# Compression's first product with the operands swapped: blocks stationary in four column groups, partial sums added and turned by one more product

## The chip, the cores and the metric

One core of one Trainium2 chip runs the whole program. The metric is device time in microseconds. TensorE does the matrix products, VectorE (DVE in rows) and ScalarE (ACT) the elementwise work, GpSimd (POOL) a little of it; SyncE (SP) issues the weight loads.

## The reference, cut to what matters

The program computes two attention layers (`hybrid_layer`), then a second block with a recurrent mixer and 16 experts. The change touches `nsa_compress`, once for keys and once for values in each of the two layers:

```
def nsa_compress(kv, pe, w1, w2):                 # kv: 1 x 256 x 2 groups x 64
    n_c = (S - 32) // 16 + 1                      # 15 blocks of 32 tokens, stride 16
    blocks = kv[:, idx] + pe[None, None, :, None, :]
    blocks = blocks.transpose(0, 1, 3, 2, 4).reshape(B, n_c, G, 32 * 64)
    return jax.nn.silu(blocks @ w1) @ w2          # w1: 2048 x 64, w2: 64 x 64
...
kc = nsa_compress(kvs("nsa_kc"), cmp_pe[0], cmp_w1[0], cmp_w2[0])
vc = nsa_compress(kvs("nsa_vc"), cmp_pe[1], cmp_w1[1], cmp_w2[1])
```

`kc` and `vc` feed the compressed branch of one of the three attention mixers (`s = einsum(qb, kc)`, a masked softmax, `o_cmp`). All is fp32.

## The kernel before, in words

Each engine runs a list of instructions in the order in which `pe_layer`, `v_layer`, `a_layer` and `pool_layer` write them down; they meet only at semaphores. `tick` and `at` name such events; `free(b)`, `fill(b)`, `drain(b)` and `drained(b)` do the same for the eight PSUM banks, so a product into bank b waits until the reader of its last content is done. Weights come as 2 MB units through a ring of four places (more in the expert stage). SP issues them in the fixed order of `unit_order`, and before each it waits until the last product on the unit that held the place is done; `take(pe)` waits for the arrival.

A layer begins with eight groups of projection columns (`cg`), each as two halves of 128 tokens (`pe_in(l, cg, t, w)`), written to banks 4 to 7 and copied to `H` by ScalarE (t=0, `a_h`) and VectorE (t=1, `v_h`). Between them TensorE turns (`pe_turn(n)`) 128x128 pieces through banks `n % 4` (turn 6 through bank 0), which ScalarE (`a_turn`) or VectorE (`v_turn`) copies to `TB`, or, for n=7, to `KC2`. Around the change the orders are:

- TensorE, `cg == 5`: `pe_in` t=0; turns 11, 12, 13; `pe_cmp1`; `pe_in` t=1; turns 3, 4, 5; then gate columns 0 (`pe_gate_cols`), `pe_cmp2`, turn 6, gate columns 1, `pe_cmp_s` (24 small products on `KCT`), then the attention pairs (`pe_attend`).
- VectorE: `v_turn` 7, `v_blocks` (adds `pe`, writes `blk`, which lies in the tile `probs`), `v_turn` 9, `v_rope_q`, `v_turn` 11 and 13, `v_cmp_hid`, `v_h` 5, `v_rope_k`, `v_turn` 3 and 5, top-k (`v_top`), `v_cmp_kv` (writes `KCT` and `VC3`), `v_sel` and so on.
- ScalarE: `a_h` 5, `a_turn` 12, `a_cmp_hid`, `a_turn` 4, `a_gates`, gate tanh 0, `a_turn` 6.

`pe_cmp1` (lines 826 to 834) runs for v = 0 (keys, bank 2) and v = 1 (values, bank 3) 16 products each (`LPAIR`, two tokens of 64 values make the 128 rows). Stationary is `w1[:, v, a, :]`, 128x64, moving is `blk[:, v, a]`, 128x30 (2 groups of 15 blocks), and the output is 64x30, hidden units on partitions. `a_cmp_hid` takes tanh(x/2) of it to `hid`, and `v_cmp_hid` makes (tanh + 1) * x in `hid2`, which `pe_cmp2` multiplies with `w2`; the factor one half comes in `v_cmp_kv`. Bank 3, for v = 1, is that of turn 11, which VectorE reads. The small constant `spread` has, in row s and column c, a one where s mod 32 = c.

A TensorE product of fp32 shows in the trace as two records. All those products go through the helper `mm`, line 648; line 798 is `pe_turn`, line 1247 `v_turn`, line 1577 `a_turn`, line 1590 `a_cmp_hid`, line 1306 `v_cmp_hid`, line 1136 `v_h`, lines 1314 and 1317 `v_cmp_kv`, line 553 SP's load of a unit, line 2181 a product of the expert stage on four column groups (`gates_T`).

Of the kernel before, what the change touches and what calls it, by code (L numbers as in the profile page):

```python
# [8 lines left out]
ALU = mybir.AluOpType  # L9
ACT = mybir.ActivationFunctionType  # L10
# [7 lines left out]
HD = 64  # L18
# [6 lines left out]
N_CMP = (SEQ - CMP_LEN) // CMP_STRIDE + 1  # L25
LPAIR = CMP_LEN // 2
# [12 lines left out]
NSA_MIX = (DSA_H + FOX_H) * HD  # L39
# [183 lines left out]
class Counts:  # L223
# [14 lines left out]
    def tick(self, name, *event, by=1):  # L238

        sem = self.sem(name)  # L240
        self.count[name] += by
        if event:
            self.events[event] = (name, self.count[name])
        return sem, by

    def last(self, name):

        return self.sem(name), self.count[name]

    def at(self, *event):  # L250

        assert event in self.events or not self.events.get("complete"), event
        name, value = self.events.get(event, ("first_building", 1))
        if name.endswith("_filled"):
            self.reading[name] = self.events["use", *event]
        return self.sem(name), value
# [4 lines left out]
    def free(self, b):  # L261

        n = self.uses.get(b, 0)
        self.uses[b] = n + 1
        return self.sem(f"bank{b}_read"), n

    def fill(self, b, *event):

        self.events["use", *event] = self.uses[b]
        return self.tick(f"bank{b}_filled", *event)  # L270

    def drain(self, b, *event):

        use = self.reading.pop(f"bank{b}_filled", None)
        assert use or not self.events.get("complete"), (b, event)
        self.done[b] = use or 1
        if event:
            self.events[event] = (f"bank{b}_read", self.done[b])
        return self.sem(f"bank{b}_read"), 1

    def drained(self, b):

        return self.sem(f"bank{b}_read"), self.done[b]


def build(nc, A, out, events):
    ctx = ExitStack()
    with ctx:
# [3 lines left out]
        def sb(name, *shape, dt=F32, stack=ctx):  # L292
            return stack.enter_context(nc.sbuf_tensor(name, [P, *shape], dt))
# [15 lines left out]
        def C(name, rows=slice(0, P)):  # L309
            lo, hi = CF[name]  # L310
            return const[rows, lo:hi]
# [59 lines left out]
        def row_of(r):  # L371
# [3 lines left out]
        PCT = rot[:, :, :].rearrange("p t n -> p (t n)")[:, 2816 - 512:2816].rearrange("p (n s) -> p n s", s=P)  # L375
        Zc = wide[:, 1, NSA_MIX:NSA_MIX + GROUPS * TILES * HPG * N_CMP].rearrange(
            "p (g t j c) -> p g t j c", g=GROUPS, t=TILES, j=HPG)
        mx = sb("mx", 3, 2, 2, stack=one)
        den = sb("den", 3, 2, 2, stack=one)
        rin = sb("rin", 3, 2, 2, stack=one)  # L380
# [266 lines left out]
        def mm(pe, o, a, b, start, stop):  # L647
            return pe.matmul(o, a, b, start=start, stop=stop)  # L648
# [177 lines left out]
        def pe_cmp1(pe, l):  # L826
            pe.wait_ge(*at("cmpw", l))
            pe.wait_ge(*at("blocks", l))
            for v in range(2):
                pe.wait_ge(*free(2 + v))  # L830
                for a in range(LPAIR):
                    ins = mm(pe, bank[2 + v][0:HD, 0:2 * N_CMP], w1[:, v, a, :],
                             blk[:, v, a, :, :].rearrange("p g c -> p (g c)"), a == 0, a == LPAIR - 1)
                ins.then_inc(*fill(2 + v, "cmp1", l, v))

        def pe_cmp2(pe, l):
            pe.wait_ge(*free(2))
            pe.wait_ge(*at("hid", l, 0))
            mm(pe, bank[2][0:HD, 0:2 * N_CMP], w2[0:HD, 0, :], hid2[0:HD, 0, :], True, True)
            pe.wait_ge(*at("hid", l, 1))  # L840
            for g in range(GROUPS):
                ins = mm(pe, bank[2][0:N_CMP, 64 * (g + 1):64 * (g + 2)], hid2[0:HD, 1, g * N_CMP:(g + 1) * N_CMP],
                         w2[0:HD, 1, :], True, True)
            ins.then_inc(*fill(2, "cmp2", l))
# [155 lines left out]
        def pe_layer(pe, l):  # L1000
            if l == 0:
                pe_open(pe)
            for cg in range(0 if l else 2, 6):
                w = take(pe, WIDTHS[cg])
                pe_in(pe, l, cg, 0, w)
                if cg == 0:
                    pe_xT(pe, l, 1)
                if cg == 3:
                    pe_index(pe, l, 0)
                if cg == 4:  # L1010
                    pe_cum(pe, l)
                if cg == 5:
                    for n in (11, 12, 13):
                        pe_turn(pe, l, n)
                    pe_cmp1(pe, l)
                pe_in(pe, l, cg, 1, w)
                if cg == 2:
                    for n in (0, 1, 2):
                        pe_turn(pe, l, n)
                    pe_gate(pe, l)  # L1020
                if cg == 3:
                    pe_index(pe, l, 1)
                if cg == 4:
                    for n in (7, 8, 9, 10):
                        pe_turn(pe, l, n)
                if cg == 5:
                    for n in (3, 4, 5):
                        pe_turn(pe, l, n)
            w = take(pe)
            pe_gate_cols(pe, l, 0, w)  # L1030
            pe_cmp2(pe, l)
            pe_turn(pe, l, 6)
            pe_gate_cols(pe, l, 1, w)
            pe_cmp_s(pe, l)
            pe_attend(pe, l, take(pe))
# [152 lines left out]
        def v_rope_k(dve, l):  # L1188
            dve.wait_ge(*at("h", l, 5, 0))
            rope(dve, COL["ks"], GROUPS, 32, plain(RKS, GROUPS, 32))  # L1190
            rope(dve, COL["kw"], GROUPS, 32, plain(RKW, GROUPS, 32), "rope", l, "k")
# [53 lines left out]
        def v_turn(dve, l, n):  # L1245
            def copy(o, i, s):
                return dve.tensor_scalar(o, i, s, None, ALU.mult) if s != 1.0 else dve.tensor_copy(o, i)  # L1247
            turn_read(dve, copy, l, n)
# [51 lines left out]

        def v_cmp_hid(dve, l):

            for v in range(2):
                dve.wait_ge(*at("hid_tanh", l, v))
                dve.wait_ge(*at("cmp1", l, v))
                dve.scalar_tensor_tensor(hid2[0:HD, v, :], hid[0:HD, v, :], 1.0,
                                                   bank[2 + v][0:HD, 0:2 * N_CMP], ALU.add, ALU.mult).then_inc(*drain(2 + v, "hid", l, v))
                dve.wait_ge(*drained(2 + v))

        def v_cmp_kv(dve, l):  # L1310
            dve.wait_ge(*at("cmp2", l))
# [176 lines left out]
        def v_layer(dve, l):  # L1488
            if l == 0:
                v_window(dve, 0)  # L1490
                for half in range(2):
                    v_ada_rows(dve, 0, half)
                    v_ada_open(dve, half)
                    v_uT(dve, 0, 0, half)
                dve.wait_ge(*at("consts", 1))
                dve.wait_ge(*at("params", 1))
            else:
                v_uT(dve, l, 1)
            v_h(dve, l, 0)
            if l:  # L1500
                dve.wait_ge(*at("lngb", l - 1))
                v_rows(dve, l, 0)
            v_h(dve, l, 1)
            if l:
                v_rows(dve, l, 1)
            else:
                v_ada_gate(dve)
            v_rope_dsa(dve, l)
            v_h(dve, l, 2)
            v_turn(dve, l, 1)  # L1510
            v_gate(dve, l)
            v_h(dve, l, 3)
            v_fox_z(dve, l)
            v_index(dve, l)
            v_top(dve, 0, P, TOPK // 8 - 2)
            v_fox_cum(dve, l)
            v_top(dve, 0, P, 2)
            v_h(dve, l, 4)
            v_turn(dve, l, 7)
            v_blocks(dve, l)  # L1520
            v_turn(dve, l, 9)
            v_rope_q(dve, l)
            v_turn(dve, l, 11)
            v_turn(dve, l, 13)
            v_cmp_hid(dve, l)
            v_h(dve, l, 5)
            v_rope_k(dve, l)
            v_turn(dve, l, 3)
            v_turn(dve, l, 5)
            v_top(dve, P, 384, TOPK // 8)  # L1530
            v_cmp_kv(dve, l)
            v_sel(dve, l)
            v_gT(dve, l, 0)
            v_cmp_z(dve, l)
            v_gT(dve, l, 1)
            if l + 1 < DEPTH:
                v_window(dve, l + 1)
            else:
                v_mod_window(dve)
            v_attend(dve, l)  # L1540
            v_ln(dve, l)
# [45 lines left out]
        def a_cmp_hid(act, l):  # L1587
            for v in range(2):
                act.wait_ge(*at("cmp1", l, v))
                act.activation(hid[0:HD, v, :], bank[2 + v][0:HD, 0:2 * N_CMP], ACT.Tanh, scale=0.5).then_inc(*tick("scalar_step", "hid_tanh", l, v))  # L1590
                act.wait_ge(*last("scalar_step"))

        def a_gates(act, l):
            act.wait_ge(*at("h", l, 5, 1))
# [1585 lines left out]
```

## Time and profile before

| | |
|---|---|
| Median of the runs | 1201.88 us (1199.24, 1201.88, 1205.79) |
| The profiled execution | 1202.91 us, span 1201.10 us, mean granted clock 0.939 |
| TensorE matmul busy | 1027.3 us (86%), 7706 records |
| TensorE weight load busy | 534.7 us (45%) |
| VectorE busy | 428.0 us (36%) |
| ScalarE busy | 236.9 us (20%) |
| GpSimd busy | 54.2 us (5%) |
| HBM read | 321.47 MB, 269 GB/s over the span |

The span is from the first to the last instruction of the profiled execution, and 1.81 us lie around it. A busy share is a mean over stages with different limits; which instructions set the end is told by the chain that is followed back from the last instruction, and by the timelines around the place of the change. A form such as `128*64 128x30` gives the stationary block's rows and columns and then the moving block. A bracket at the end of a row gives the engine's idle time before it and what ended that.

### The profile page before, as it was taken

To read this page: it belongs to the slowest core of one execution; us is meant where nothing else is said; L and a number is where in the kernel's file an instruction comes from. 1 tells how busy PE (TensorE), PEld (TensorE's weight loads), DVE (VectorE), ACT (ScalarE), POOL (GpSimd) and SP (SyncE) were. 2 spreads that over 40 slices of the span, in tenths; PEclk is the share of its full clock that TensorE was granted. 3 is DMA by queue.
4 is the path that set the end of the run, shared out by engine and by line. 5 is a ranking of instruction groups with operands and counts; after the bars stand their busy time and mean duration, and the time that the engine had idled before them with its cause. 6 is when DMAs were issued, how large, how long until landed. Compare 5 with 4: busy or idle time off the path is not lost.

```text
span 1201.1 us, 18162 instructions
## 1 busy us (share of the span) xinstructions
PE 1027.3 (86%) x7706; PEld 534.7 (45%) x7706; DVE 428.0 (36%) x1023; ACT 236.9 (20%) x587; POOL 54.2 (5%) x70
## 2 busy tenths in 40 slices
PE   5999999999999989999988889998666666666667
PEld 2344774444477446885657765432111111111112
DVE  0137646333775527445238783411000000000002
ACT  0011135111213423444113352200000000000002
POOL 0101000000100000000222400000000000000000
PEclk9999989999999999999999999899888888879779
DMA  9973238553325994013222016999999999999996
GB/s 383 404 280 141 86 133 331 188 193 141 140 78 225 426 385 165 1 70 141 81 98 108 5 72 244 411 416 432 428 431 430 428 431 431 429 430 429 431 429 275
DMA packets 28159, 323.68 MB, mean 269 GB/s; under 512 B 3264, under 2 KB 3392, under 8 KB 5808
## 3 DMA queue, kind: packets, MB, share of 16 engines
q1 hardware_dynamic: 26048, 314.18, 63.8%
q0 software_dynamic: 2032, 8.35, 2.0%
q8 instruction: 61, 1.00, 0.3%
q14 instruction: 18, 0.15, 0.0%
HBM read 321.47 MB, written 1.05 MB: 269 GB/s over the span
## 4 chain that ended last, share of the span: by engine, by line
PE 60%; DMA 31%; DVE 4%; issue 2%; ACT 1%; SPq 1%; DVEq 0%; ACTq 0%
PE banks L648 49%; DMA zuv_to_Kt<-in_stream 17%; DMA ring<-in_stream 14%; PE banks L659 3%; PE banks L2195 1%; PE banks L911 1%; PE banks L897 1%; PE banks L932 1%; SPq L553 1%; PE banks L894 1%; PE banks L798 1%; DVE KC L1247 0%; PE banks L902 0%; PE banks L935 0%; DVE probs L1297 0%
## 5 line engine op out<-in xcount | busy, mean ns | idle before, releaser
L648 PE MATMUL banks<-ring,uT 128*128 128x512 f32 (+1 forms) x512 | 226.4, 597 | 7.2 <-DMA ring<-in_stream 4.2
L648 PEld LDWEIGHTS banks<-ring,uT 128*128 128x128 f32 x512 | 96.3, 192 | 121.6 <-issue 112.5
L648 PE MATMUL banks<-ring,scr_qk 128*32 128x512 f32 (+1 forms) x496 | 86.6, 655 | 23.2 <-DMA ring<-in_stream 22.7
L648 PE MATMUL banks<-ring,UWK 128*32 128x512 f32 (+1 forms) x336 | 87.8, 795 | 15.9 <-ACT UWK L3051 9.3
L648 PE MATMUL banks<-scr_qk 64*64 64x64 f32 (+2 forms) x2368 | 80.4, 260 | 21.8 <-DMA scr_qk<-in_stream 15.4
L2761 DVE SCALAR_TENSOR_TENSOR UWK<-UWK,banks 128x256 f32<-128x256 f32 x16 | 6.7, 421 | 259.0 <-ACT UWK L3043 259.0
L3043 ACT ACTIVATE UWK<-banks 128x256 f32<-128x256 f32 x16 | 6.1, 383 | 361.2 <-PE banks L648 361.2
L648 PEld LDWEIGHTS banks<-scr_qk 64*64 64x64 f32 (+2 forms) x2368 | 54.6, 132 | 46.3 <-issue 34.6
L648 PE MATMUL banks<-UWK,ring 128*128 128x256 f32 x320 | 71.0, 380 | 0.0
L648 PEld LDWEIGHTS banks<-UWK,ring 128*128 128x128 f32 x320 | 60.4, 190 | 9.3 <-issue 1.4
L2195 PE MATMUL banks<-UWK 128*128 128x512 f32 x128 | 63.7, 620 | 0.9 <-DVE UWK L2769 0.9
L648 PE MATMUL banks<-uT,ring 128*128 128x256 f32 x256 | 59.3, 392 | 0.0
L659 PE MATMUL banks<-ring,KC 128*32 128x512 f32 x384 | 47.3, 617 | 13.8 <-DMA ring<-in_stream 13.8
L648 PEld LDWEIGHTS banks<-ring,scr_qk 128*32 128x32 f32 (+1 forms) x496 | 24.5, 124 | 72.9 <-issue 47.2
L648 PEld LDWEIGHTS banks<-ring,UWK 128*32 128x32 f32 (+1 forms) x336 | 27.3, 152 | 61.2 <-issue 49.9
L648 PEld LDWEIGHTS banks<-uT,ring 128*128 128x128 f32 x256 | 50.2, 199 | 7.1
L2769 DVE TENSOR_TENSOR UWK<-banks,grow 128x512 f32<-128x512 f32 x16 | 11.1, 692 | 109.7 <-PE banks L648 109.7
L1616 ACT ACTIVATE probs<-banks,mx 128x128 f32<-128x128 f32 x88 | 36.6, 418 | 41.9 <-DVE mx L1384 37.9
L2195 PEld LDWEIGHTS banks<-UWK 128*128 128x128 f32 x128 | 21.8, 190 | 47.4 <-issue 45.1
L1136 DVE COPY H<-banks 128x512 f32<-128x512 f32 (+1 forms) x12 | 8.2, 681 | 84.5 <-PE banks L648 84.5
L648 PE MATMUL banks<-const,scr_qk 64*64 64x64 f32 (+1 forms) x208 | 20.2, 448 | 20.9 <-DMA misc<-in_stream 20.9
L648 PE MATMUL banks<-Vt_to_O,UWK 128*64 128x128 f32 (+1 forms) x208 | 23.1, 504 | 9.2 <-DVE Vt_to_O L2524 2.7
(380 smaller groups left out, 1223.6 us busy)
## 6 DMA issues: line engine op xcount, KB each, us to landing
ring<-in_stream SPq DMA_DIRECT2D x93, 2048.0 KB, 14.4
scr_qk<-in_stream SPq DMA_DIRECT2D x11, 2048.0 KB, 40.1
Vt_to_O<-in_stream SPq DMA_DIRECT2D x11, 2048.0 KB, 39.6
zuv_to_Kt<-in_stream SPq DMA_DIRECT2D x10, 2048.0 KB, 40.1
scr_qk<-in_stream SPq DMA_DIRECT2D x11, 1024.0 KB, 40.9
wide<-in_stream SPq DMA_DIRECT2D x10, 1024.0 KB, 38.5
const<-in_stream SPq DMA_DIRECT2D x10, 1024.0 KB, 37.4
misc<-in_stream SPq DMA_DIRECT2D x10, 1024.0 KB, 39.6
```

The source lines that it names most:

```text
L553: sp.dma_start(held(slot[k]), A["stream"][k, :, :]).then_inc(*tick(f"arrived{slot[k]}", by=16))
L648: return pe.matmul(o, a, b, start=start, stop=stop)
L659: ins = pe.matmul(bank[b][32 * j:32 * j + 32, :], window[:, j * (DCH // 4) + k, lo:lo + 32], w[:, j * (DCH // 4) + k, :], start=(n, k) == ...
L798: ins = pe.transpose(bank[b][0:rows, (2 * m + t) * P:(2 * m + t + 1) * P], f(t), ident)
L894: pe.matmul(bank[b + s][:, 0:P], q[:, 0:P], k[:, 0:P], start=True, stop=False)
L897: pe.matmul(bank[b + s][:, P:384], q[:, P:SEQ], k[:, :], start=False, stop=False)
L911: ins = pe.transpose(bank[4 + s][:, i * P:(i + 1) * P], probs[:, m % 3, s, i * P:(i + 1) * P], ident)
L932: pe.matmul(bank[6][HD * s:HD * s + HD, 0:SEQ], H[:, 0, v:v + HD], probT[:, m % 2, s, 0:SEQ], start=first and kind != "slc", stop=False)
L1136: dve.tensor_copy(H[:, 1, AT[cg]:AT[cg] + WIDTHS[cg]], bank[b][:, 0:WIDTHS[cg]]).then_inc(*drain(b, "h", l, cg, 1))
L1616: ins = act.activation(probs[:, i, s, lo:hi], bank[b + s][:, lo:hi], ACT.Exp, bias=mx[:, i, s, t:t + 1], accum_out=den[:, i, s, t:t + 1])
L2195: ins = pe.matmul(bank[2 * t + h], PgT[:, t, :], ye[:, h, 0:512], start=e == 0, stop=e == EXPERTS - 1)
L2769: dve.tensor_tensor(ye[:, 0, 0:512], bank[4], grow[:, 0:512], ALU.mult).then_inc(*drain(4, "ye", e, 0))
```

## The change

`pe_cmp1` swaps the operands. Stationary is now a block of 32 columns of the flat `probs` (the 30 of `blk[:, v, a]` and the first two of the next, 30 only for the very last), moving is `w1[:, v, a, :]`, 64 columns. Product a goes to column group j = a % 4, so to partitions 32j to 32j+31 of the bank and its columns 0 to 63, and four products add up in each group. The output has blocks on partitions and hidden units along them, in four partial sums. ScalarE copies both banks to `cmp_part` (in the tile `wide`). A new product, `pe_cmp1_sum`, for each v has `cmp_part[:, v, :]` stationary (128x64) and 30 columns of `spread` moving: that adds the four parts and turns the result, so that it is 64x30 again, for both v in bank 2 (`hid_rows`). TensorE runs it between the second half of the projection and turns 3 to 5. The tanh and the (tanh + 1) * x are one instruction each now, over both v; the tanh waits for the sum, and `v_cmp_hid` moves behind `v_rope_k`. No DMA is added, removed or moved.

```diff
@@ -375,6 +375,8 @@
         PCT = rot[:, :, :].rearrange("p t n -> p (t n)")[:, 2816 - 512:2816].rearrange("p (n s) -> p n s", s=P)
         Zc = wide[:, 1, NSA_MIX:NSA_MIX + GROUPS * TILES * HPG * N_CMP].rearrange(
             "p (g t j c) -> p g t j c", g=GROUPS, t=TILES, j=HPG)
+        cmp_part = wide[:, 1, NSA_MIX:NSA_MIX + 2 * HD].rearrange("p (v n) -> p v n", v=2)
+        hid_rows = bank[2][0:HD, 0:64].rearrange("p (v n) -> p v n", v=2)[:, :, 0:2 * N_CMP]
         mx = sb("mx", 3, 2, 2, stack=one)
         den = sb("den", 3, 2, 2, stack=one)
         rin = sb("rin", 3, 2, 2, stack=one)
@@ -829,15 +831,24 @@
             for v in range(2):
                 pe.wait_ge(*free(2 + v))
                 for a in range(LPAIR):
-                    ins = mm(pe, bank[2 + v][0:HD, 0:2 * N_CMP], w1[:, v, a, :],
-                             blk[:, v, a, :, :].rearrange("p g c -> p (g c)"), a == 0, a == LPAIR - 1)
+                    j, r = a % 4, a // 4
+                    lo = (v * LPAIR + a) * 2 * N_CMP
+                    n = 2 * N_CMP if (v, a) == (1, LPAIR - 1) else 32
+                    ins = mm(pe, bank[2 + v][32 * j:32 * j + n, 0:HD], pflat[:, lo:lo + n], w1[:, v, a, :],
+                             r == 0, r == LPAIR // 4 - 1)
                 ins.then_inc(*fill(2 + v, "cmp1", l, v))
+
+        def pe_cmp1_sum(pe, l):
+            pe.wait_ge(*free(2))
+            for v in range(2):
+                pe.wait_ge(*at("cmp_part", l, v))
+                ins = mm(pe, bank[2][0:HD, 32 * v:32 * v + 2 * N_CMP], cmp_part[:, v, :], C("spread")[:, 0:2 * N_CMP], True, True)
+            ins.then_inc(*fill(2, "cmp_sum", l))
 
         def pe_cmp2(pe, l):
             pe.wait_ge(*free(2))
-            pe.wait_ge(*at("hid", l, 0))
+            pe.wait_ge(*at("hid", l))
             mm(pe, bank[2][0:HD, 0:2 * N_CMP], w2[0:HD, 0, :], hid2[0:HD, 0, :], True, True)
-            pe.wait_ge(*at("hid", l, 1))
             for g in range(GROUPS):
                 ins = mm(pe, bank[2][0:N_CMP, 64 * (g + 1):64 * (g + 2)], hid2[0:HD, 1, g * N_CMP:(g + 1) * N_CMP],
                          w2[0:HD, 1, :], True, True)
@@ -1024,6 +1035,7 @@
                     for n in (7, 8, 9, 10):
                         pe_turn(pe, l, n)
                 if cg == 5:
+                    pe_cmp1_sum(pe, l)
                     for n in (3, 4, 5):
                         pe_turn(pe, l, n)
             w = take(pe)
@@ -1300,12 +1312,10 @@
 
         def v_cmp_hid(dve, l):
 
-            for v in range(2):
-                dve.wait_ge(*at("hid_tanh", l, v))
-                dve.wait_ge(*at("cmp1", l, v))
-                dve.scalar_tensor_tensor(hid2[0:HD, v, :], hid[0:HD, v, :], 1.0,
-                                                   bank[2 + v][0:HD, 0:2 * N_CMP], ALU.add, ALU.mult).then_inc(*drain(2 + v, "hid", l, v))
-                dve.wait_ge(*drained(2 + v))
+            dve.wait_ge(*at("hid_tanh", l))
+            dve.wait_ge(*at("cmp_sum", l))
+            dve.scalar_tensor_tensor(hid2[0:HD, :, :], hid[0:HD, :, :], 1.0, hid_rows, ALU.add, ALU.mult).then_inc(*drain(2, "hid", l))
+            dve.wait_ge(*drained(2))
 
         def v_cmp_kv(dve, l):
             dve.wait_ge(*at("cmp2", l))
@@ -1522,9 +1532,9 @@
             v_rope_q(dve, l)
             v_turn(dve, l, 11)
             v_turn(dve, l, 13)
-            v_cmp_hid(dve, l)
             v_h(dve, l, 5)
             v_rope_k(dve, l)
+            v_cmp_hid(dve, l)
             v_turn(dve, l, 3)
             v_turn(dve, l, 5)
             v_top(dve, P, 384, TOPK // 8)
@@ -1587,8 +1597,10 @@
         def a_cmp_hid(act, l):
             for v in range(2):
                 act.wait_ge(*at("cmp1", l, v))
-                act.activation(hid[0:HD, v, :], bank[2 + v][0:HD, 0:2 * N_CMP], ACT.Tanh, scale=0.5).then_inc(*tick("scalar_step", "hid_tanh", l, v))
-                act.wait_ge(*last("scalar_step"))
+                act.activation(cmp_part[:, v, :], bank[2 + v][:, 0:HD], ACT.Copy).then_inc(*drain(2 + v, "cmp_part", l, v))
+            act.wait_ge(*at("cmp_sum", l))
+            act.activation(hid[0:HD, :, :], hid_rows, ACT.Tanh, scale=0.5).then_inc(*tick("scalar_step", "hid_tanh", l))
+            act.wait_ge(*last("scalar_step"))
 
         def a_gates(act, l):
             act.wait_ge(*at("h", l, 5, 1))
```

## Rows read from the trace of the kernel before

**Rows 1.** The page, chain that ended last, shares by engine and line.

```profile
PE 60%; DMA 31%; DVE 4%; issue 2%; ACT 1%; SPq 1%; DVEq 0%; ACTq 0%
```

**Rows 2.** The chain in order of time: start us, us, what.

```profile
122.10 0.70 DVE TB L1247
122.84 8.26 PE banks L648 x48
131.10 1.31 PE banks L798 x12
...
840.65 5.91 SPq L553
```

**Rows 3.** TensorE timeline, layer 0: start us, us, engine, line, what.

```profile
120.49 2.05 PE L648 MATMUL banks<-probs,w 128*64 128x30 f32 x32
122.84 2.05 PE L648 MATMUL banks<-probs,w 128*64 128x30 f32 x32 [0.30 <-DVE TB L1247]
124.82 6.28 PE L648 MATMUL banks<-ring,uT 128*128 128x448 f32 x16
...
139.25 0.30 PE L648 MATMUL banks<-hid,w 64*64 64x30 f32 x2
139.48 0.39 PE L648 MATMUL banks<-w,hid 64*15 64x64 f32 x4
139.80 0.66 PE L798 MATMUL banks<-const,rot 128*128 128x128 f32 x4
...
147.30 2.43 PE L648 MATMUL banks<-KCT,TB 64*128 64x15 f32 x24
```

**Rows 4.** TensorE timeline, the same place in layer 1.

```profile
334.04 2.05 PE L648 MATMUL banks<-probs,w 128*64 128x30 f32 x32 [0.29 <-DVE TB L1247]
336.02 6.28 PE L648 MATMUL banks<-ring,uT 128*128 128x448 f32 x16
```

**Rows 5.** Busy time by stretch, the last stretch: stretch, length, engines, clock, DMA, GB/s.

```profile
840.00:1201.00 361.00, 244.74 (x1488) 63.97 (x1480) 31.77 (x60) 19.84 (x50) 0.00 (x0) 0.84 0.98 417
```

**Rows 6.** Waits of the SP queue, 440 to 850: us, times, longest.

```profile
SPq L553 <- PE banks L648: 284.0, 28, 48.2
```

**Rows 7.** TensorE timeline, a burst of the expert stage.

```profile
773.33 0.65 PE L2181 MATMUL banks<-const,scr_qk 128*32 128x128 f32 x16
```

**Rows 8.** Groups by line and form, TensorE: busy us, mean ns, idle before.

```profile
L2181 PE MATMUL banks<-const,scr_qk 128*32 128x128 f32 x256 | 10.0, 273 | 0.0
...
L648 PE MATMUL banks<-KCT,TB 64*128 64x15 f32 x48 | 4.9, 260 | 0.0
```

**Rows 9.** ScalarE timeline, layer 0.

```profile
122.62 1.28 ACT L1590 ACT_TABLE_LOAD   x1 [1.81 <-PE banks L648]
...
124.99 0.19 ACT L1590 ACTIVATE hid<-banks 64x30 f32<-64x30 f32 x1 [0.89 <-PE banks L648]
132.07 0.60 ACT L1577 ACTIVATE TB<-banks 128x512 f32<-128x512 f32 x1 [6.90 <-PE banks L798]
```

**Rows 10.** VectorE timeline, layer 0.

```profile
124.20 0.18 DVE L1306 SCALAR_TENSOR_TENSOR hid<-hid,banks 64x30 f32<-64x30 f32 x1 [0.69 <-ACT hid L1590]
...
131.21 0.62 DVE L1136 COPY H<-banks 128x448 f32<-128x448 f32 x1 [5.76 <-PE banks L648]
...
135.29 1.42 DVE L1247 TENSOR_SCALAR TB<-banks 128x512 f32<-128x512 f32 x2
...
145.74 0.36 DVE L1314 TENSOR_SCALAR KCT<-banks 64x15 f32<-64x15 f32 x2
```

**Rows 11.** Busy time by stretches of 1 us, columns as in rows 5.

```profile
150.00:151.00 1.00, 1.00 (x6) 0.91 (x5) 0.90 (x5) 0.00 (x0) 0.00 (x0) 0.50 0.84 360
...
156.00:157.00 1.00, 1.00 (x4) 0.84 (x3) 0.00 (x0) 0.08 (x1) 0.00 (x0) 0.65 0.00 0
```

**Rows 12.** Busy time by stretches of 10 us, columns as in rows 5.

```profile
120.00:130.00 10.00, 9.70 (x84) 6.94 (x82) 3.69 (x10) 2.25 (x4) 0.00 (x0) 1.00 0.01 2
...
360.00:370.00 10.00, 10.00 (x48) 8.48 (x47) 4.39 (x16) 2.29 (x9) 0.78 (x1) 0.83 0.78 295
```

## The prediction

> **What bounds the kernel now.** I read the chain that ended last first, since the change touches two short stretches and the question is whether they lie on it. TensorE has 60% of it, the weight stream 31%, VectorE 4% [rows 1]. In order of time the chain goes, in layer 0, from VectorE's read of turn 11 (122.10, 0.70 us) to 48 TensorE records from 122.84 on [rows 2]. By TensorE's timeline these 48 are 32 of the second compression product (v=1) and 16 of the second half of the sixth projection group [rows 3]. So only v=1 is on the chain. v=0 starts at 120.49 and is done by 122.54; then TensorE waits 0.30 us for bank 3, which VectorE empties at 122.80. Whatever v=0 saves is added to that wait. Layer 1 has the same pattern 211.2 us later: v=1 at 334.04, the projection at 336.02 [rows 4].
>
> The second question is whether time won there reaches the end. The end is bound by the stream: from 840 to 1201 us the 16 DMA engines are busy 0.98 of the time, TensorE 245 of 361 us [rows 5]. But SP issues each load only when a ring place is free, and what it waits for is TensorE: 284.0 us in 28 waits between 440 and 850 [rows 6], and the chain itself passes through such an SP issue at 840.65 [rows 2]. No clock time is fixed after the compression; every load behind it is released by a program event that moves with TensorE. So a gain is passed on nearly whole, and a loss too. It is only small beside the span.
>
> **What v=1 costs, before and after.** Before: v=1 starts at 122.84 and the projection behind it at 124.82, 1.98 us for 32 records (16 fp32 products, two records each), 62 ns a record; 1.98 us in layer 1 as well [rows 3, 4]. Each has 64 stationary columns and 30 moving ones. After: again 16 products in 32 records, each with 32 stationary columns and 64 moving ones, four column groups in turn. The trace has no such form. The nearest is the expert stage's small burst on four column groups, 32 stationary and 128 moving: 16 records in 0.65 us, the mean duration of one 0.273 us, so starts lie (0.65 - 0.27) / 15 = 25 ns apart [rows 7, 8]. That is far under what 128 columns cost alone: the 12 full-width transposes of turns 3 to 5, 128 columns each, take 1.31 us on the chain, 109 ns each [rows 2]. So four groups do stream side by side. With half the moving columns the spacing should be no longer, but here each product also brings new weights, where the burst repeats one block on four groups. Bounds: 25 ns below (the burst), 62 ns above (the present form, which has twice the stationary columns and no overlap of groups). I take 30, near the burst, because it shares the groups and the stationary width. v=1 then takes 32 x 30 = 0.96 us, 1.02 less than now. At 25 it is 1.18 less, at 62 nothing.
>
> A rule speaks against this. The Trainium skill, TensorE: Matmul & The Clock Gate, section "The mechanism" (Part 3), says that a weight load overlaps matmuls in flight only where the row group differs, and all four column groups here use the same 128 rows. By its "LDWEIGHTS" section a load of 32 columns is an estimated 27 ns, and a record would take that and its streaming in series, about 80 ns; the sum by it is 32 x 80 = 2.6 us, 0.6 more than now, against my 1.0 less. The burst's 25 ns [rows 7] disagrees for repeated weights.
>
> **The added summing product.** `pe_cmp1_sum` puts four records (two products, 64 stationary and 30 moving columns, the old form) between the projection and turns 3 to 5, on the chain. At 62 ns they are 0.25 us. They also change the array's tiling twice. The nearest row is the second compression product: six small records with both changes of tiling take from 139.25 to 139.80, 0.55 us [rows 3]. Bounds 0.25 and 0.55; I take 0.40, since four of six records are there with both changes. Their waits cost nothing: v=1's copy out of PSUM by ScalarE is at most a 0.2 us instruction (0.19 us for the tanh of 30 columns [rows 9], 64 columns are a little more, say 0.22) and is done by about 124.1, and the projection covers it until 130. If that cover were gone, the sum would wait some 0.3 us.
>
> **ScalarE.** Two copies are added, two tanhs become one, and the tanh moves behind the sum: it waits until about 130.5 (turn 3 starts at 131.10 now [rows 2], so the sum at 130.08, and it takes 0.40). In front of it stands the table load, 1.28 us, which before fell at 122.62 in ScalarE's idle time. Table load and a tanh of 60 columns (0.25 us) end at about 132.1; then comes turn 4's read, which ran at 132.07 before [rows 9] and could now run at 131.5, were ScalarE free. So it stays where it was; the next who needs it is turn 6 on bank 0, TensorE at 139.80, 7 us later. Behind it come `a_gates` and the first gate tanh, which waits for gate columns that TensorE finishes before 139.25 [rows 3], so they have the same cover. Nothing is late.
>
> **VectorE.** `v_cmp_hid` leaves the idle stretch after turn 13 (its two instructions were 0.18 us each) and becomes one instruction over 64x60 behind `v_rope_k`, in VectorE's busiest stretch: 0.2 us, with its wait and hand-over 0.25. It needs the tanh (132.1) and comes at about 134.3, so it does not wait. Queued behind it are turns 3 and 5 (135.29), top-k and `v_cmp_kv`; the last KCT write ends at 146.10 [rows 10]. TensorE begins the products on KCT at 147.30, a margin of 1.20 us [rows 3]. VectorE's stretch starts at the copy of the projection (131.21 [rows 10]), which moves 1.02 earlier with TensorE; less 0.25 it is 0.77 earlier. TensorE arrives 0.62 earlier. The margin becomes 1.35; it would decide only if the new VectorE work cost over 1.6 us. `pe_cmp2` needs the result at about 138.6, 4 us after it is there. POOL and SP get no new work. `cmp1`, for which POOL's next load of `w1` waits, comes earlier, with a layer between.
>
> **Sum.** Per layer 0.40 - 1.02 = -0.62 us; two layers -1.2. The profiled execution took 1202.91 us, 1.81 over its span of 1201.10, and it is 1.03 over the median of 1201.88. Span 1199.9, own time 1201.7, median 1200.7. By the bounds, the best is 2 x (0.25 - 1.18) = -1.9 (1200.0) and the worst 2 x 0.55 = +1.1 (1203.0).
>
> **Rivals.**
> (1) Weight loads and matmuls of the four groups run in series, so that nothing overlaps. From rows: 128 stationary and 15 moving columns take (2.43 - 0.26) / 23 = 94 ns in the KCT product [rows 3, 8], 64 and 30 take 62. Taking off the streaming (0.85 ns a column, from 109 ns for 128) leaves 81 and 36 ns of load, so 32 columns perhaps 16, and 64 moving columns add 54: 70 ns. v=1 is 2.24 us, with the sum +0.66 a layer: 1203.2. The four-group burst at 25 ns is against it. 10%. The rule of the Trainium skill above would bring this case about.
> (2) The clock falls inside the compression; this one ends slower. The granted clock is 1.00 (2.4 GHz) now through 120 to 130 us. But after the 24 tiny KCT products that begin at 147.30 it is 0.50 (1.2 GHz) from 150 on and back within 156 to 157 (0.65, so at about 156.7), and in layer 1 there is a shorter drop (0.83 over 360 to 370, 3.4 us of it low) [rows 11, 12]. After the change v=0 ends at about 121.6, TensorE is idle for 1.2 us, then works for 1 us in small matmuls: less work in the array than before. If the clock falls for 6.7 us over the projection, 3.4 us are lost. In one layer 1204.1, in both 1207.5. It decides from the first such drop, since 3.4 is over five times the gain of a layer. Against it: the present 4.3 us with a wait trigger none. 10%, of which 4 for both.
> (3) The drops at 150 and 361 us go away, because TensorE's pattern before them moves: 3.4 + 1.7 = 5.1 us won, 1195.6. The KCT burst just ahead of both is unchanged, which speaks against. 8%.
> (4) The gain is absorbed by a wait that I don't see, in the mixed stretch of 160 to 430 us, where a load may come as late as before: 1201.9. The loads there are released by TensorE too. 10%.
>
> **How the numbers follow.** The forecast holds 62%: 1200.7, its own range 1197.5 to 1204.0, the bounds (1200.0 to 1203.0) and some of the scatter of the runs shown, 1199.24 to 1205.79. For 8 in 10 I take 1196.5 to 1205.5, which takes in rivals 1 and 4 and the one-layer case of 2, and leaves out two-layer drops and rival 3. About 0.5%, 6 us, is what a measurement of this kernel can tell from no change. Faster by more needs rival 3 and luck: 5%. Slower by more needs rival 2 in both layers, or scatter on one: 6%. Within: 89%.
>
> **What would show it.** In the changed profile: v=1 starts where turn 11's read ends, its 32 records of 128*32 take 0.8 to 1.2 us, and the wait before it grows from 0.30 to about 1.2; four records of form 128*64 stand before turn 3, 0.3 to 0.5 us from the projection to turn 3; the table load stands after the sum, and turn 4's read directly behind the tanh; VectorE's hid instruction follows rope without idle time; `KCT` is still ready before TensorE asks. From the start of v=1 to the start of the KCT products, now 24.46 us, I expect 23.8. Records over 62 ns, a granted clock under 1.00 from 120 to 140, or an idle TensorE ahead of the sum would make the prediction wrong.

## The result, and the profile after

The changed kernel takes 1197.25 us (median of 20 executions, 1192.05 to 1203.51), the kernel before 1205.22 (20 executions, 1199.24 to 1209.32). The ratio is 0.9941, 95% interval 0.9928 to 0.9954. That is inside the range of the forecast (1196.5 to 1205.5), but it is 7 us of gain where I had worked out 1.2, and it lies just beyond the half per cent, where I had given 5%.

That the time lies inside the range is luck. I worked from a median of 1201.88 of three executions, and twenty executions of the same kernel have 1205.22. Measured from 1201.88, the range allows a gain of at most 5.4 us; by the ratio the gain is 7.1 (5.5 to 8.7), so it lies outside. My 1.2 us taken off 1205.22 would have been 1204.0.

The profile after has the same chain as before, share by share, TensorE 60% and the stream 31% [rows 1]. TensorE's timeline of it in layer 0, in the columns of [rows 3] (line 650 is the helper `mm`, line 800 the turns):

```profile
120.62 0.65 PE L650 MATMUL banks<-w,probs 128*32 128x64 f32 x32
122.98 0.65 PE L650 MATMUL banks<-w,probs 128*32 128x64 f32 x32 [1.70 <-DVE TB L1259]
123.56 6.28 PE L650 MATMUL banks<-ring,uT 128*128 128x448 f32 x16
129.77 0.42 PE L650 MATMUL banks<-const,wide 128*64 128x30 f32 x4
130.12 0.87 PE L800 MATMUL banks<-const,rot 128*128 128x128 f32 x6
...
146.53 2.43 PE L650 MATMUL banks<-KCT,TB 64*128 64x15 f32 x24
```

v=1's 32 records run from 122.98 to the projection at 123.56: 0.58 us against 1.98, or 18 ns a record with the hand-over to the projection. Before it TensorE waits 1.70 us instead of 0.30, so v=0's gain is lost there as expected. The sum takes 0.35 us (129.77 to 130.12). From v=1's start to the KCT products it is 23.55 us, before 24.46 [rows 3]: 0.91 us won in this layer. The repeated profile of the changed kernel (`e4_after_again`) has 23.56 us in layer 0, where 23.5 was expected.

In layer 1 of the same execution the 1.4 us of v=1 are eaten up by the clock:

```profile
333.24 0.65 PE L650 MATMUL banks<-w,probs 128*32 128x64 f32 x32 [1.70 <-DVE TB L1259]
333.82 7.98 PE L650 MATMUL banks<-ring,uT 128*128 128x448 f32 x16
341.73 0.42 PE L650 MATMUL banks<-const,wide 128*64 128x30 f32 x4
```

The projection takes 7.91 us here instead of 6.21 in layer 0. Busy time by stretch says why; the column before the last two is the granted clock, 1.00 in layer 0 and 0.83 in layer 1, which is 3.4 us of the ten at the lower level (1.2 GHz):

```profile
120.00:130.00 10.00, 8.30 (x91) 4.60 (x88) 3.49 (x10) 2.35 (x5) 0.00 (x0) 1.00 0.00 0
...
330.00:340.00 10.00, 8.30 (x85) 4.68 (x84) 3.69 (x9) 2.61 (x5) 0.00 (x0) 0.83 0.00 0
```

ScalarE in layer 0 (line 1600 the new copy, 1602 the tanh, 1587 a turn's read; compare [rows 9]):

```profile
123.70 0.22 ACT L1600 ACTIVATE wide<-banks 128x64 f32<-128x64 f32 x1 [2.07 <-PE banks L650]
123.94 1.28 ACT L1602 ACT_TABLE_LOAD   x1
130.23 0.21 ACT L1602 ACTIVATE hid<-banks 64x60 f32<-64x60 f32 x1 [5.00 <-PE banks L650]
131.31 0.60 ACT L1587 ACTIVATE TB<-banks 128x512 f32<-128x512 f32 x1 [0.87 <-PE banks L800]
```

VectorE in layer 0 (line 1148 the projection's copy, 1317 `v_cmp_hid`, 1259 turn 3 and 5, 1324 KCT; compare [rows 10]):

```profile
129.95 0.62 DVE L1148 COPY H<-banks 128x448 f32<-128x448 f32 x1 [6.31 <-PE banks L650]
...
134.03 0.21 DVE L1317 SCALAR_TENSOR_TENSOR hid<-hid,banks 64x60 f32<-64x60 f32 x1
134.27 1.42 DVE L1259 TENSOR_SCALAR TB<-banks 128x512 f32<-128x512 f32 x2
...
144.73 0.36 DVE L1324 TENSOR_SCALAR KCT<-banks 64x15 f32<-64x15 f32 x2
```

The two profiled executions have spans of 1201.10 and 1200.4 us. They differ by 0.7 us where the medians differ by 8 (the profiled execution of the changed kernel, 1202.21 us, is the second slowest of its 20), so this pair alone can't show where the time came from. The question for the experiments was why a cut of about 2 us on the chain is worth 7.

### The profile page after: what moved, and what is told of

It is laid out like the page before. It is cut to its first block, busy times and chain, and to the rows that moved or that the text cites. A ratio compares the mean times of both kernels' runs of the same rounds, so it can differ in the third digit from the quotient of the medians.

```text
span 1200.4 us, 18176 instructions
## 1 busy us (share of the span) xinstructions
PE 1018.7 (85%) x7714; PEld 530.7 (44%) x7714; DVE 428.3 (36%) x1021; ACT 237.5 (20%) x589; POOL 54.3 (5%) x70
## 3 DMA queue, kind: packets, MB, share of 16 engines
HBM read 321.47 MB, written 1.05 MB: 269 GB/s over the span
## 4 chain that ended last, share of the span: by engine, by line
PE 60%; DMA 31%; DVE 4%; issue 2%; ACT 1%; SPq 1%; DVEq 0%; ACTq 0%
PE banks L650 49%; DMA zuv_to_Kt<-in_stream 17%; DMA ring<-in_stream 14%; PE banks L661 3%; PE banks L2207 1%; PE banks L922 1%; PE banks L908 1%; PE banks L943 1%; SPq L555 1%; PE banks L905 1%; PE banks L800 1%; DVE KC L1259 0%; PE banks L913 0%; PE banks L946 0%; DVE probs L1309 0%
## 5 line engine op out<-in xcount | busy, mean ns | idle before, releaser
L650 PE MATMUL banks<-ring,scr_qk 128*32 128x512 f32 (+1 forms) x496 | 82.6, 621 | 28.6 <-DMA ring<-in_stream 28.0
L650 PE MATMUL banks<-scr_qk 64*64 64x64 f32 (+2 forms) x2368 | 84.6, 267 | 23.4 <-DMA scr_qk<-in_stream 19.1
```

## The experiments

In what follows the chain's gain of the change is 1.05 us a layer (1.40 for v=1, less 0.35 for the sum), 2.1 in all.

**Is it the time on TensorE, or something else in the change?** The first run gives the time back and leaves all else as changed.

```diff
                              r == 0, r == LPAIR // 4 - 1)
+                if v == 1:
+                    for a in range(9):
+                        ins = mm(pe, bank[3][0:HD, 128:128 + 2 * N_CMP], w1[:, v, a, :],
+                                 blk[:, v, a, :, :].rearrange("p g c -> p (g c)"), True, True)
                 ins.then_inc(*fill(2 + v, "cmp1", l, v))
```

> The changed kernel, with nine more products in the old form (64 stationary, 30 moving columns) behind v=1's, written to columns of bank 3 that nobody reads: 18 records, about 1.1 us on the chain in each layer, so that the projection starts about when it did before. Theory P (the time comes from the chain: 1.05 us a layer less, and the rest of the measured -7 us is scatter): ratio to before 1.000. Theory C (the change makes the clock drops of later stages fewer or cheaper, through what TensorE does here): the pad gives TensorE its old work and its old time back, ratio 1.000 too. Theory D (something else in the change, on ScalarE or VectorE, is worth the rest): ratio about 0.995 to 0.996.

Measured: ratio to the kernel before 0.9993 (0.9970 to 1.0017), 1202.72 us. The gain is gone. The timeline of this run shows the pad at 1.38 us in layer 0, so that the projection starts 1.97 us after v=1, as before. But part of that is the clock, which is 0.70 from 123 to 124 and 0.50 from 124 to 126 in this execution. In layer 1 the 18 records take 1.17 us at the full clock (337.27 to 338.44), 65 ns each, and with them and the sum the layer is 0.1 us longer than before.

```profile
121.97 0.65 PE L650 MATMUL banks<-w,probs 128*32 128x64 f32 x32 [1.70 <-DVE TB L1263]
122.56 1.45 PE L650 MATMUL banks<-probs,w 128*64 128x30 f32 x18
123.94 7.69 PE L650 MATMUL banks<-ring,uT 128*128 128x448 f32 x16
```

The second run is the reverse: the kernel before, with only the time taken out.

```diff
-                for a in range(LPAIR):
+                n = LPAIR if v == 0 else 7
+                for a in range(n):
                     ins = mm(pe, bank[2 + v][0:HD, 0:2 * N_CMP], w1[:, v, a, :],
-                             blk[:, v, a, :, :].rearrange("p g c -> p (g c)"), a == 0, a == LPAIR - 1)
+                             blk[:, v, a, :, :].rearrange("p g c -> p (g c)"), a == 0, a == n - 1)
```

> The kernel before, with 9 of the 16 products of v=1 left out (so the compressed values are not the reference's): 18 records of 62 ns, 1.1 us less on the chain in each layer, nothing else changed. Theory P: v=1 then takes 0.87 us, ratio 0.998. Theory S (a shift of all that follows by 1 us a layer is worth more than itself, because of what it meets later): ratio about 0.994, as the change. Theory D: 0.998 at the most, since the change's other parts are absent.

Measured: ratio 0.9954 (0.9933 to 0.9976), 1198.47 us. v=1 takes 0.93 us in it (122.13 to 123.06), 1.05 less than before, the chain's gain of the change exactly:

```profile
122.13 1.00 PE L648 MATMUL banks<-probs,w 128*64 128x30 f32 x14 [0.30 <-DVE TB L1248]
123.06 6.28 PE L648 MATMUL banks<-ring,uT 128*128 128x448 f32 x16
```

So theory D falls: the copies, the moved `v_cmp_hid`, the joint tanh and the column groups as such aren't needed for the gain. It comes with the time taken from TensorE at this place. And theory P falls in its narrow form, since 2.1 us on the chain gave 5.5 us here (2.9 to 8.1). These two runs leave theory C (the clock) and theory S (the shift meets something later).

**Does the result repeat?** Both kernels were run again, unchanged.

> The kernel before once more, unchanged: how far two runs of the same program lie apart, and a second profile of it, to see which clock drops and which stages repeat. All theories: ratio 1.000 within 0.2%; before 840 us five to nine low stretches of the clock, at different places from the first profile except near the end of the KCT products.

> The changed kernel once more, unchanged. Theory P: its ratio falls from 0.994 towards 0.998. Theories C, D and S: 0.994 again. In its profile v=1 to the KCT products takes 23.5 us if no clock drop falls into it, 1.7 more for each drop of 3.4 us.

Measured: the kernel before again 1.0015 (0.9997 to 1.0032), the changed one again 0.9944 (0.9921 to 0.9968). The 7 us are no scatter. In the repeated profile of the kernel before, the clock is low around the compression, where the first profile had 1.00 (compare [rows 12]):

```profile
120.00:130.00 10.00, 9.70 (x61) 6.12 (x60) 2.09 (x5) 1.66 (x3) 0.00 (x0) 0.83 0.01 2
...
330.00:340.00 10.00, 9.71 (x83) 7.43 (x81) 4.74 (x14) 2.80 (x5) 0.00 (x0) 0.75 0.00 0
340.00:350.00 10.00, 10.00 (x41) 6.87 (x40) 4.06 (x14) 0.83 (x2) 0.00 (x0) 0.91 0.35 111
```

It is at 1.2 GHz for 3.4 us of 120 to 130, and for 5 and 1.8 us of the two stretches in layer 1. Before 840 us it has nine low stretches. I had expected them at other places than in the first profile, but six of the nine are within 5 us of one of the first (150, 362, 433, 607, 648 and 751 us there); those at 123, 174 and 335 are new. Such falls come and go from one execution to the next with the same program, and rival 2's event happens without the change as well.

Every execution has its span and its mean granted clock, so the time at the low level can be worked out as 2 x (1 - clock) x span. Over all full executions of both programs in all comparisons (one at 2563.77 us left out), with standard errors (on three chips, between which the mean span of the kernel before varies from 1202.7 to 1204.9 us):

| | executions | mean span, us | low time, us |
|---|---|---|---|
| kernel before | 72 | 1203.6 +- 0.4 | 135.6 +- 1.2 |
| changed kernel | 32 | 1195.6 +- 0.6 | 126.4 +- 1.7 |

The changed kernel spends 9 us less at 1.2 GHz. Most of the low time lies in the stream-bound expert stage, where it costs little: from 840 on the clock is 0.84 in [rows 5]. Accordingly, from one full execution to the next the span grows by only 0.18 us for each us of low time (0.19 in the kernel before, 0.17 in the changed one). At that price 9 us are worth 1.7.

**Where is the gain made?** To split off the expert stage, both kernels were run with 4 of 16 experts.

```diff
+RUN = 4
...
-    for e in range(EXPERTS):
+    for e in range(RUN):
...
-            for e in range(1, EXPERTS):
-                end = e == EXPERTS - 1
+            for e in range(1, RUN):
+                end = e == RUN - 1
```

and the same in `v_experts`, `a_experts`, `a_final` and the last products.

> The kernel before, which runs 4 of the 16 experts (24 of the 96 expert units are loaded, the output is not the reference's), so that it ends some 300 us earlier, soon after the stage bound by TensorE. To be compared with the next run. Theory P' (2.1 us from the chain, the other 5 us from the long stream-bound expert stage): this and the next differ by 2 to 3 us. Theory C (the other 5 us come from fewer low stretches of TensorE's clock where TensorE is the limit, before 840 us): they differ by 5 to 7 us, and the low time of the clock differs by about 8 us.

> The changed kernel with 4 of 16 experts (output not the reference's). Theory P': 2 to 3 us under the run before it. Theory C: 5 to 7 us under it, with about 8 us less low clock.

> The kernel before with 4 of 16 experts again, since the first pair had 6 and 5 executions only and differed by 4.2 us, of which 2.0 is half of the difference in low clock time. If all of the 7 us are there before the long expert stage, this pair differs by 6 to 8 us; if 2 to 3 us come in that stage, by 4 to 5.

> The changed kernel with 4 of 16 experts again: 4 to 5 us under the run before it if the first pair was typical, 6 to 8 if the expert stage adds nothing, 2 if only the chain counts.

Measured: medians 855.95 and 851.64 us, in the second pair 856.01 and 850.06. So the first pair differs by 4.3 us, between the 2 to 3 of theory P' and the 5 to 7 of theory C, and the second by 6.0. Both pairs together:

| | executions | mean span | low time | span less half the low time |
|---|---|---|---|---|
| before, 4 experts | 11 | 853.8 +- 1.0 | 36.7 +- 2.2 | 835.5 +- 0.2 |
| changed, 4 experts | 10 | 848.8 +- 0.9 | 31.4 +- 2.5 | 833.1 +- 0.6 |

The last column is what each execution would have taken at the full clock, if TensorE were the limit throughout. For the kernel before it takes nearly all scatter out (span and low time correlate at 0.98), for the changed one a third. The span grows by 0.44 us for each us of low time in the one and by 0.33 in the other, so a microsecond at 1.2 GHz costs a little less than half a microsecond in this part of the program. What is left between the two is 2.4 +- 0.6 us, the chain's 2.1 (3.0 if the common slope of 0.38 is used in place of a half). The spans themselves differ by 5.0 +- 1.3, and the other 2.6 are half of 5.2 us less low time (+- 3.3, so taken alone this part isn't certain).

The profiled executions of this set can't show the clock's part, because they disagree. In the second pair the clock up to 440 us is 0.98 in both kernels, and then the changed one has the higher; here are the stretches of the kernel before and of the changed one:

```profile
440.00:830.00 390.00, 359.95 (x4057) 240.91 (x4059) 186.29 (x348) 113.27 (x241) 38.62 (x35) 0.96 0.42 165
440.00:830.00 390.00, 362.90 (x4115) 240.70 (x4113) 186.33 (x349) 113.68 (x242) 38.55 (x35) 0.98 0.43 169
```

In the first pair it is the other way round: 1.00 and 0.98 before, 0.98 and 0.98 changed, with spans of 846.3 and 850.2 us.

What all profiled executions do show is the two parts of the program apart, with an elementwise product of VectorE for the second expert as a mark. It is there in every kernel that has experts, in the first profile of the kernel before at 796.77:

```profile
796.77 0.42 DVE L2764 TENSOR_TENSOR UWK<-UWK,banks 128x256 f32<-128x256 f32 x1
```

| one profiled execution each | mark at, us | low time before it | mark less half of that | mark to end |
|---|---|---|---|---|
| before; again | 796.77; 801.05 | 30.7; 41.0 | 781.4; 780.6 | 404.3; 403.0 |
| before, 4 experts; again | 791.11; 800.28 | 17.1; 37.5 | 782.6; 781.5 | |
| changed; again | 795.33; 795.36 | 30.7; 30.7 | 780.0; 780.0 | 405.1; 404.3 |
| changed, 4 experts; again | 793.63; 791.99 | 27.3; 27.3 | 780.0; 778.3 | |
| change with the pad | 800.01 | 34.1 | 782.9 | 404.4 |
| 9 of 16 left out | 795.79 | 34.1 | 778.7 | 404.4 |
| 15 of 16 left out | 789.69 | 23.9 | 777.7 | 404.4 |
| 9 products repeated | 800.88 | 30.7 | 785.5 | 403.0 |

(The last two are of the experiments further below.) Less half the low time, the changed kernel reaches the mark 2.0 +- 0.6 us earlier in the mean of four, the chain's 2.1. From the mark to the end all eight full executions take 403.0 to 405.1 us, whatever the kernel and whatever the 91.5 to 121.8 us of low time behind the mark. So low time there costs nothing that shows, and in these executions nothing is won there.

A second cut ends both kernels after the two layers and writes their result.

```diff
-            for k in range(len(units)):
+            for k in range(44):
...
-                    sp.wait_ge(*at("result", t, h))
+                    sp.wait_ge(*at("x_new", DEPTH, t))
...
-            pe_streams(pe)
-            pe_chunks(pe, 0)
...
```

and so on for everything behind the layers on each engine.

> The kernel before, which ends after the two attention layers and writes their result (everything of the second block, and the loads for it, left out), at about 500 us. To be compared with the next run. Chain alone: they differ by 2.1 us (1.05 a layer) once half of the low clock time is taken off each. If the change also makes low stretches fewer or shorter inside the layers, the low time differs too, by up to 8 us, and the medians by 4 to 6.

> The changed kernel, ended after the two layers in the same way. Chain alone: 2.1 us under the run before it, with equal low time. With the clock as well: 4 to 6 us under.

Measured: medians 478.88 us (5 executions) and 474.75 (4). Mean spans 477.1 +- 0.4 and 473.3 +- 0.9, low time 20.6 +- 1.2 and 16.3 +- 0.7, spans less half the low time 466.8 +- 0.4 and 465.1 +- 0.7. So 1.7 us by the chain (of 2.1) and 2.1 by the clock. The difference in low time, 4.3 us, is about three standard errors here, with nine executions in all. The profiles don't bear it out: up to one VectorE instruction near the end of the layers (at 471.83 in the first profile) the kernel before has 17.1, 23.9, 3.4, 13.7 and 14.2 us of low time in its five profiles, the changed one 20.5, 20.5, 13.7, 13.7 and 13.7. That less low time arises in the two layers is suggested, not shown.

**Is each microsecond worth three?** Two more amounts, on the kernel before: v=1 with 1 product of 16 (v=1 takes 0.23 us, 1.75 less a layer), and v=1 with its first 9 products repeated.

```diff
-                for a in range(LPAIR):
+                n = LPAIR if v == 0 else 1
+                for a in range(n):
...
-                             blk[:, v, a, :, :].rearrange("p g c -> p (g c)"), a == 0, a == LPAIR - 1)
+                             blk[:, v, a, :, :].rearrange("p g c -> p (g c)"), a == 0, a == n - 1)
```

> The kernel before, with 15 of the 16 products of v=1 left out (the compressed values are not the reference's): 30 records of 62 ns, 1.86 us less a layer on the chain, 3.7 in all. If only the chain counts: ratio 0.997. If each microsecond of shift were worth three, as 9 products left out seem to say (2.2 us on the chain, 5 us measured): 0.991. If the first 1 us a layer reaches a better position and more does not help (a position effect): 0.993 to 0.995.

```diff
-                for a in range(LPAIR):
-                    ins = mm(pe, bank[2 + v][0:HD, 0:2 * N_CMP], w1[:, v, a, :],
-                             blk[:, v, a, :, :].rearrange("p g c -> p (g c)"), a == 0, a == LPAIR - 1)
+                n = LPAIR if v == 0 else LPAIR + 9
+                for a in range(n):
+                    ins = mm(pe, bank[2 + v][0:HD, 0:2 * N_CMP], w1[:, v, a % LPAIR, :],
+                             blk[:, v, a % LPAIR, :, :].rearrange("p g c -> p (g c)"), a == 0, a == n - 1)
```

> The kernel before with v=1's first 9 products repeated (the compressed values are not the reference's): 18 records, 1.1 us more a layer, 2.2 in all. If only the chain counts: ratio 1.002. If each microsecond is worth three: 1.005. If it is a position effect, anything between 0.996 and 1.004.

Measured: 0.9912 (0.9882 to 0.9942; 1195.81 us, 6 executions) and 0.9988 (0.9969 to 1.0007; 1205.59 us). All amounts in one table. The chain's column is for both layers at the full clock; that of the repeated products is 36 records at 62 ns (in its profile v=1 takes 3.64 and 4.04 us, at the low clock for a part of each).

| | chain, us | measured against before, us | low time, us |
|---|---|---|---|
| 15 of 16 left out | -3.5 | -10.6 (-14.3 to -7.0) | 125 +- 5 |
| the change | -2.1 | -7.1 (-8.7 to -5.5) | 126 +- 2 |
| 9 of 16 left out | -2.1 | -5.5 (-8.1 to -2.9) | 124 +- 3 |
| the kernel before | 0 | | 136 +- 1 |
| the change with the pad | +0.2 | -0.8 (-3.6 to +2.0) | 133 +- 4 |
| 9 products repeated | +2.2 | -1.4 (-3.7 to +0.8) | 137 +- 3 |

On the side of the cuts each microsecond gives about three. On the side of the additions 2.2 us give nothing that can be measured, and the interval leaves out the 6.6 us that three to one would ask. So it is no constant factor. The low time follows the same step: about 125 us with any of the cuts, 133 to 137 without. This would fit a position effect through the clock, that is, one that depends on when the work arrives and not on how much was saved. But it isn't shown: the two sides differ by only 10 us of low time, whose half is 5 us at the most, and most of that time lies behind the mark, where it costs nothing.

## Why the prediction was right, and where not

**The place on the chain** was right. v=1 counts and v=0 doesn't: the wait before v=1 grew by 1.40 us and ate v=0's gain.

**The price of a record** was mis-sized: 18 ns measured, where I took 30 out of 25 to 62. The lower bound itself was too high, and it mixed two measures: 25 ns counts starts only, while 62 and 18 take in the hand-over to the next product. By starts only the new records lie (0.65 - 0.22) / 31 = 14 ns apart (0.22 us is the mean duration of one). In the trace they come in rounds of four, one for each column group, 56 ns from round to round. The burst of [rows 7], with twice the moving columns, has 109 ns from round to round, as long as 128 columns take alone. So the streaming of the moving columns set the burst's spacing, and with half of them it is half. v=1 takes 0.58 us, not 0.96. The sum cost 0.35 us, not 0.40. So a layer's term is -1.05 and not -0.62 us. From v=1's start to the KCT products 0.91 remain, since the projection and what follows were 0.14 us slower (6.21 against 6.12, and 16.41 against 16.36).

**Rival 1**, loads and matmuls in series at 70 ns, is refuted by the same 18 ns, now with new weights in each product. By the rule of the Trainium skill (TensorE: Matmul & The Clock Gate, "The mechanism"), which I had weighed, a load overlaps matmuls in flight only where the row group differs, and my estimate from it was 80. Measurement and rule differ, and the measurement decides.

**ScalarE and VectorE** cost nothing, as predicted. The table load was not where I put it: it follows the second copy at 123.94, in idle time, and not the sum. So turn 4's read came at 131.31, 0.76 us earlier than before, where I had it unmoved. VectorE's new instruction took 0.21 us at 134.03 and KCT was done at 145.09, 1.44 us before TensorE's products on it (forecast 1.35).

**"So a gain is passed on nearly whole, and a loss too"** is the step that failed. 2.1 us on the chain became about 7 at the end. The chain's own part does arrive whole: with 4 experts the clock-corrected difference is 2.4 us, and at the mark near 797 us it is 2.0. What failed is the assumption that nothing comes on top of it. With 4 experts 2.6 +- 1.7 us go with less time at 1.2 GHz, which is the most that the runs show of a cause, and it is not certain. I had the clock only as two rivals with whole falls, at 10% and 8%, judged by one execution each. Rival 3 ("the drops go away", 1195.6) was nearest to the measured time, but by luck: the drops at 150 and 361 us that I named are still there in both profiles of the changed kernel. What may change is how often such falls come over many executions, and a single profile can't tell that. The forecast sum was made as if the low time were a constant.

**What stays open.** First, whether and why less work at this place means fewer low stretches. The profiles show them at many places (125, 150, 174, 334, 361, 433, 607, 645, 750 us), one or two at each, in some executions and not in others; that is too few profiles for a count. Second, the remaining part. Full programs differ by 8.0 +- 0.7 us in mean span, those cut to 4 experts by 5.0 +- 1.3. The 3.0 +- 1.5 between them are not seen behind the mark in any profile (403.0 to 405.1 us), so they are scatter, or something that the few profiled executions don't catch; both profiled full executions of the changed kernel are 4 to 5 us slower than its mean. Third, why the additions cost nothing. In their profiles they do cost up to the mark: less half the low time it comes at 785.5 us with the repeated products and at 782.9 with the pad, against 780.6 to 782.6 before, and the mean over the executions doesn't show it.

## What to carry to other kernels

Small products with at most 32 columns on one side can gain from making that side stationary, spread over the four column groups: here the cost per product fell by a factor of 3.4, and a product with a 0/1 matrix adds up and turns the parts for 0.35 us. Where the clock moves between two levels, compare many executions, and where TensorE is the limit take half of each one's low time off before you judge a change of a microsecond. With 4 experts that took the standard error of the mean from 1.0 to 0.2 us for the kernel before and from 0.9 to 0.6 for the changed one. It doesn't help for the full program, where most of the low time costs nothing (0.35 us without it, 0.45 with it). Don't take a baseline from three executions when you forecast a microsecond: here it was 3.3 us off. And when a change leaves something off the chain, test its worth by padding the new kernel and cutting the old one by the same amount, before you credit its parts.

## What the runs showed of the hardware that I had not expected

Records of 32 stationary and 64 moving columns in fp32, on four column groups with new weights each time, cost 18 ns each (0.58 us for 32). The same work as 64 stationary and 30 moving columns costs 62 ns a record. The matmuls start in rounds of four, 7 ns apart within a round and 56 ns from round to round. The weight loads have records of 106 to 109 ns, and those of a round start 7 ns apart too, so the loads of different column groups overlap each other and the matmuls in flight.

A ScalarE table load needn't wait for the operand of its activation: here it ended 5.0 us ahead of the tanh, behind the copy, while before it started only when the operand was there (122.62, 0.08 us after v=0's last record). Which of the two happens wasn't tested.
